# Second attention divided behind its value products, and the first mixer's sigmoids read from the banks

## The chip, the core and the metric

The program runs on one core of a Trainium2 chip. The metric is the device time of one execution in microseconds (us), lower is better. A core has a matrix engine (TensorE, PE in the profile, with its weight loads as PEld), three engines for elementwise work (VectorE or DVE, ScalarE or ACT, GpSimd or POOL), and a queue that issues the transfers (SyncE or SP). The matrix engine writes into eight banks of 128 x 512 f32. Each engine works through its own instructions in order and meets the others only at semaphores.

## What is computed

Two transformer blocks run one after the other on 512 tokens of width 1024. The first has a gated FFN, a token mixer (four recurrent heads, `_hgrn2`, beside a spatial gating), a cross attention over 256 memory tokens, and a second FFN. The second block has a mixer of self attention and pooling, and an FFN. Two pieces are touched.

The gates of the first mixer, in the reference:

```
log_f = jnp.log(lb + (1.0 - lb) * jax.nn.sigmoid(fz))
k = (1.0 - lb) * jax.nn.sigmoid(-fz)
b = jnp.cumsum(lfc, axis=2)            # within chunks
```

The self attention of the second block, 8 query heads of 64 over 2 key and value heads:

```
s = jnp.einsum('bqkgd,bskd->bkgqs', qblk, k).astype(jnp.float32) * scale
p = jax.nn.softmax(s, axis=-1)
return jnp.einsum('bkgqs,bskd->bqkgd', p.astype(v.dtype), v)
```

## The kernel before

**Linear layers.** Each weight is used as a high part (`whi`, cast by ScalarE, L394) and a low part (`wlo`, a subtraction by VectorE or GpSimd, L399; `lo_owner` at L359 says by which). A block is 128 output columns: eight products with the high part and the high activation (L434), eight with the low activation (L435), and eight with the low part of the weight (L438). Blocks run through banks 0 to 3. Each block has a place in one list (`blocks`), and the casts and splits run three blocks ahead (`AHEAD`).

**First mixer.** Its input layer (`in`, 24 blocks) begins with the four forget projections FZ0 to FZ3, which are multiplied in halves together with the layer norm in front. `plan` (L660) lists for each block which small steps follow it; each engine has a function `mixer` with its own part of each step. For a head: VectorE copies the bank to `mk` (L1787). ScalarE takes two sigmoids of it, L1059 into `cum` and L1060 into `mk`. VectorE makes forget gate and key (L1694 to L1696). ScalarE takes the logarithm (L1065, after `use_logs`, L1001, which loads another table). VectorE scans (L1700). GpSimd makes the arguments of the decays (L1298, L1299) and ScalarE their exponential (L1069). VectorE scales query and key by them (L1665 into `qt`, L1667 into `kt`), and the matrix engine multiplies these (L2206), for 7 levels and the diagonal. The first two such products stand behind block 5 (IV0) in the matrix engine's order, the next two behind block 6, and so on.

VectorE's order at the start, before: copies of blocks 0 to 2, between them the low parts of blocks 4 and 5; the gates of head 0 ahead of the copy of block 3; then the gates of heads 1, 2 and 3, the scan of head 0, the copy of block 4 (Q0), and the first scaling. GpSimd splits block 6 at its step 3 and block 7 at its step 4, behind the arguments of levels 0 and 1.

**Second attention.** Before its loop the layer `in2` (10 blocks) makes keys, queries, values and the pooled input; the scores of head 0 stand behind block 8. In turn h of the loop the matrix engine does: scores of tiles 0 and 1 of head h+1 (L2369, L2370); transposes of columns 0 and 1 of head h's probabilities (`self_turn`, L2418); scores 2; value products 0 and 1 of head h-1 (`self_attend`, L2430); scores 3; transposes 2 and 3; value products 2 and 3. In turns 2 to 5 the product of one pooling group follows (L2453). VectorE takes each tile's maximum (L1903), ScalarE the exponential with the row's sum (L1177), and VectorE inverts the sum (L1911) and multiplies the probabilities by it in place (L1912). Only then are they transposed (wait on `s_pn`). VectorE copies one transposed column out of the bank (L1964), ScalarE three (L1211). The value product of a head fills 64 of a bank's 128 partitions, so two heads share a bank; after the second of them ScalarE writes the high part `ahi` (L1217) and VectorE the low part `alo` (L1969), both from the bank. `out2` takes these tiles in the order `OUT2_TILES`. GpSimd pools (L1348 to L1352) during the first turns.

Of the kernel before, what the change touches and what calls it, by code (L numbers as in the profile page):

```python
# [92 lines left out]
def build(nc, A, out):  # L93
    ctx = ExitStack()
    with ctx:
# [116 lines left out]
        sv = take("sv", [P, TT, P])  # L212
# [6 lines left out]
        po = rope  # L219
        take = region(0)  # L220
# [352 lines left out]
        s_sig = sem("gates_sigmoid")  # L573
# [54 lines left out]
        s_ah = sem("attended_hi")  # L628

# [31 lines left out]
        for h in range(HG):  # L661
            plan[1 + h] += [("forget", h)]
        plan[4] += [("logs", 0)]
# [81 lines left out]
        OUT2_TILES = [0, 7, 1, 6, 5, 2, 4, 3]  # L745
# [101 lines left out]
        def _(act):  # L847
# [208 lines left out]
            def mixer(kind, n):  # L1056
                if kind == "forget":
                    wait_in(act, FZ0 + n)
                    link(act.activation(cum[:, n, :], mk[:, n, :], ACT.Sigmoid))  # L1059
                    act.activation(mk[:, n, :], mk[:, n, :], ACT.Sigmoid, scale=-1.0).then_inc(s_sig, 1)  # L1060
                elif kind == "logs":
                    use_logs()
                    for h in range(HG):
                        act.wait_ge(s_fg, h + 1)
                        act.activation(cum[:, h, :], cum[:, h, :], ACT.Ln).then_inc(s_lf, 1)  # L1065
# [103 lines left out]
            def self_exp(h, t):  # L1169
# [7 lines left out]
                act.activation(ps[:, h % 2, t, :], score_bank(n)[:, :], ACT.Exp, bias=small[:, c:c + 1],  # L1177
                               accum_out=small[:, S_SM + n % 8:S_SM + n % 8 + 1]).then_inc(s_pe, 1)
# [33 lines left out]

            def attended_hi(h):

                if h % 2:
                    act.wait_ge(s_pv, 2 * XH + h + 1)
                    act.copy(ahi[:, h // 2, :], bank[6 + (h // 2) % 2][:, :]).then_inc(s_ah, 1)  # L1217

            for h in range(QH):
                if h >= 2:  # L1220
                    attended_hi(h - 2)
                self_exp(h + 1, 0)
                self_exp(h + 1, 1)
                if 0 <= h - POOL_AT - 1 < 4:
# [3 lines left out]
                take_transposed(h, 1)  # L1228
                self_exp(h + 1, 2)
                self_exp(h + 1, 3)  # L1230
                take_transposed(h, 2)
                take_transposed(h, 3)
# [125 lines left out]
        def _(dve):  # L1358
# [330 lines left out]
            def mixer(kind, n):  # L1689
                if kind == "forget":  # L1690

                    lb, oml = small[:, S_LB + n:S_LB + n + 1], small[:, S_OML + n:S_OML + n + 1]
                    dve.wait_ge(s_sig, n + 1)
# [76 lines left out]
            GATES = {3: (("forget", 0),), 4: (("forget", 1), ("forget", 2), ("forget", 3), ("scan", 0))}  # L1770
# [5 lines left out]
            for n, tasks in enumerate(plan):  # L1776
                for task in GATES.get(n, ()):
                    mixer(*task)
                for task in tasks:
                    if task[0] not in ("forget", "logs"):  # L1780
# [5 lines left out]
                wait_block(dve, phases["in"], n)  # L1786
                dve.tensor_copy(IN_DST[n], bank_of(phases["in"], n)[:, :]).then_inc(bank_free, 1)  # L1787
# [117 lines left out]
            def self_normalise(h, t):  # L1905
                n = TT * h + t
                c = n % 8
                if h >= QH:
                    return
                dve.wait_ge(s_pe, TT * XH + n + 1)  # L1910
                link(dve.reciprocal(small[:, S_RI + c:S_RI + c + 1], small[:, S_SM + c:S_SM + c + 1]))  # L1911
                dve.tensor_scalar(ps[:, h % 2, t, :], ps[:, h % 2, t, :], small[:, S_RI + c:S_RI + c + 1], None, ALU.mult).then_inc(s_pn, 1)  # L1912

            def prepare(kind, j):
                if kind == "softmax":
                    for t in range(TT):
                        self_max(0, t)
                        if t:
# [556 lines left out]
```

## Time and profile before

| | |
|---|---|
| median of three runs | 1740.86 us (1740.73 to 1741.76) |
| the profiled execution | 1740.76 us, of which its span is 1738.9 us |
| busy in the span | PE 1701.5 us (98%), DVE 681.1 (39%), ACT 589.5 (34%), POOL 710.9 (41%) |
| mean granted clock of the matrix engine | 0.996 |
| longest waits of the matrix engine for another engine | 4.1 us in the first mixer, 3.4 us in the second attention |

The busy share of a matrix engine's row counts matmuls at a lower clock as busy, too. In a timeline, rows of one line that follow each other are merged (x8), the time behind them runs to the end of the last, and matmuls overlap: the start of the next row tells how long the engine was taken. Square brackets give the idle time before a row and what ended it.

### The profile page before, as it was taken

The page shows a single profiled execution, that of the slowest core. Times are in us where ns is not written, and L with a number is a line of the kernel's source. Part 1 is how long each engine was busy: PE and PEld are TensorE (multiplying, and loading weights), DVE is VectorE, ACT ScalarE, POOL GpSimd, SP SyncE. Part 2 cuts the span into 40 slices and gives each one's busy share as a digit, 9 for nine tenths or more (in the row PEclk, how much of TensorE's full clock was granted, in tenths as well). Part 3 has the DMA queues.
Part 4 walks back from the last instruction along what each step waited for, and adds up shares of the span by engine and source line. Part 5 has one row for each costly group of instructions (what it writes and reads, how often), then busy time and mean ns, then how long its engine had stood idle before and what let it go on. Part 6 is the DMA issues. An engine that isn't in the chain of part 4 may idle for free.

```text
span 1738.9 us, 21093 instructions
## 1 busy us (share of the span) xinstructions
PE 1701.5 (98%) x8525; PEld 1417.6 (82%) x8525; DVE 681.1 (39%) x1122; ACT 589.5 (34%) x890; POOL 710.9 (41%) x386
## 2 busy tenths in 40 slices
PE   7999999998999999999999999999899999999998
PEld 6888888897888789879888888898657988888886
DVE  3111211268776776356211121266884522112122
ACT  4222222256444554236222222246453422222210
POOL 3443444445554343114453444433331454444442
PEclk9999999999999999999999999999999999999999
DMA  6333243333222345212433233342111333323322
GB/s 189 97 97 97 79 116 97 97 110 85 61 61 61 97 125 142 73 49 71 112 97 97 82 112 97 86 128 61 37 37 49 85 98 97 97 82 112 97 85 73
DMA packets 302826, 157.66 MB, mean 91 GB/s; under 512 B 5145, under 2 KB 301194, under 8 KB 302730
## 3 DMA queue, kind: packets, MB, share of 16 engines
q1 hardware_dynamic: 302730, 156.32, 31.6%
q8 instruction: 68, 1.11, 0.3%
q14 instruction: 28, 0.23, 0.1%
HBM read 154.20 MB, written 2.10 MB: 90 GB/s over the span
## 4 chain that ended last, share of the span: by engine, by line
PE 66%; DVE 4%; ACT 3%; issue 2%; POOL 0%; DVEq 0%; ACTq 0%; POOLq 0%
PE bank L434 16%; PE bank L435 16%; PE bank L438 15%; PE bank L2430 1%; PE bank L2054 1%; PE bank L2051 1%; PE bank L2050 1%; PE bank L481 1%; PE bank L482 1%; PE bank L486 1%; PE bank L2206 1%; PE bank L467 1%; PE bank L461 1%; PE bank L462 1%; PE bank L2311 1%
## 5 line engine op out<-in xcount | busy, mean ns | idle before, releaser
L399 POOL TENSOR_TENSOR wlo<-wraw,whi 128x1024 fp32r<-128x1024 f32 (+1 forms) x256 | 608.6, 2390 | 909.9 <-ACT whi L394 909.9
L434 PE MATMUL bank<-ahi,whi 128*128 128x512 f32 x1312 | 516.0, 393 | 0.0
L435 PE MATMUL bank<-alo,whi 128*128 128x512 f32 x1312 | 511.7, 390 | 0.0
L394 ACT CAST whi<-wraw 128x1024 fp32r<-128x1024 f32 (+1 forms) x286 | 285.9, 1025 | 255.4 <-PE bank L438 169.4
L438 PE MATMUL bank<-ahi,wlo 128*128 128x512 f32 x1312 | 324.0, 389 | 0.0
L434 PEld LDWEIGHTS bank<-ahi,whi 128*128 128x128 f32 x1312 | 247.2, 188 | 52.1 <-issue 1.2
L435 PEld LDWEIGHTS bank<-alo,whi 128*128 128x128 f32 x1312 | 247.0, 188 | 52.0 <-issue 1.2
L438 PEld LDWEIGHTS bank<-ahi,wlo 128*128 128x128 f32 x1312 | 246.3, 188 | 51.1
L1377 DVE SCALAR_TENSOR_TENSOR hval<-gate,bank 128x512 f32<-128x512 f32 x66 | 45.4, 688 | 557.2 <-PE bank L438 543.2
L859 ACT ACTIVATE gate<-bank 128x512 f32<-128x512 f32 x66 | 39.6, 600 | 514.9 <-PE bank L438 506.1
L1386 DVE SCALAR_TENSOR_TENSOR res<-res,bank 128x512 f32<-128x512 f32 x80 | 54.1, 686 | 261.7 <-PE bank L438 181.7
L434 PE MATMUL bank<-hid,whi 128*128 128x512 f32 x332 | 130.5, 393 | 0.0
L435 PE MATMUL bank<-hid,whi 128*128 128x512 f32 x332 | 129.9, 391 | 0.0
L438 PE MATMUL bank<-hid,wlo 128*128 128x512 f32 x332 | 83.4, 391 | 0.0
L438 PEld LDWEIGHTS bank<-hid,wlo 128*128 128x128 f32 x332 | 62.3, 188 | 13.7
L434 PEld LDWEIGHTS bank<-hid,whi 128*128 128x128 f32 x332 | 62.4, 188 | 13.4
L435 PEld LDWEIGHTS bank<-hid,whi 128*128 128x128 f32 x332 | 62.4, 188 | 13.4
L1368 DVE TENSOR_TENSOR hid<-hval,hid 128x512 fp32r<-128x512 f32 x66 | 67.2, 1019 | 2.3
L876 ACT ACTIVATE gate<-res 128x256 f32<-128x256 f32 (+1 forms) x48 | 23.4, 488 | 120.5 <-DVE res L1386 66.7
L2050 PE MATMUL bank<-ahi,whi 128*128 128x256 f32 x256 | 63.3, 285 | 0.0
L2051 PE MATMUL bank<-alo,whi 128*128 128x256 f32 x256 | 62.8, 283 | 0.0
L481 PE MATMUL bank<-hid,whi 128*128 128x512 f32 x132 | 52.0, 394 | 0.0
(304 smaller groups left out, 2241.7 us busy)
## 6 DMA issues: line engine op xcount, KB each, us to landing
wraw<-in_ffn_w_gate SPq DMA_DIRECT2D x44, 512.0 KB, 3.8
wraw<-in_ffn_w_up SPq DMA_DIRECT2D x44, 512.0 KB, 3.8
wraw<-in_w_in SPq DMA_DIRECT2D x34, 512.0 KB, 3.9
wraw<-in_ffn_w_down SPq DMA_DIRECT2D x32, 512.0 KB, 4.0
wraw<-in_w_gate SPq DMA_DIRECT2D x22, 512.0 KB, 3.8
wraw<-in_w_up SPq DMA_DIRECT2D x22, 512.0 KB, 3.8
wraw<-in_w_out SPq DMA_DIRECT2D x16, 512.0 KB, 4.4
wraw<-in_w_down SPq DMA_DIRECT2D x16, 512.0 KB, 4.0
```

Source lines behind the costliest of these rows:

```text
L394: eng.copy(whi[:, b % 4, 0:n], wraw[:, b % RAW, 0:n]).then_inc(hi_ready, 1)
L399: eng.tensor_tensor(wlo[:, b % RAW, 0:n], wraw[:, b % RAW, 0:n], whi[:, b % 4, 0:n], ALU.subtract).then_inc(LO[b][0], 1)
L434: eng.matmul(o, w, xhi[:, k, :], start=(k == 0), stop=False)
L435: eng.matmul(o, w, xlo[:, k, :], start=False, stop=False)
L438: mm = eng.matmul(o, wlo[:, b % RAW, k * P:(k + 1) * P], xhi[:, k, :], start=False, stop=(k == ph.K - 1))
L481: eng.matmul(o, whi[:, b % 4, k * P:(k + 1) * P], hhi[:, k, :], start=(k == 0), stop=False)
L859: act.activation(gate[:, tile % 2, :], bank_of(ph, j)[:, :], ACT.Silu).then_inc(gate_done, 1)
L1368: dve.tensor_tensor(hlo[:, at, :], hval[:, tile % 2, :], hhi[:, at, :], ALU.subtract).then_inc(hidden_ready, 1)
L1377: dve.scalar_tensor_tensor(out=hval[:, tile % 2, :], in0=gate[:, tile % 2, :], scalar=scale, in1=bank_of(ph, j)[:, :], op0=ALU.mult, op1=A ...
L1386: dve.scalar_tensor_tensor(out=res[:, j, :], in0=res[:, j, :], scalar=scale, in1=bank_of(ph, j)[:, :], op0=ALU.mult, op1=ALU.add).then_inc ...
L2050: pe.matmul(o, w, xhi[:, k, at], start=(k == 0), stop=False)
L2051: pe.matmul(o, w, xlo[:, k, at], start=False, stop=False)
```

## The change

Second attention: the probabilities are transposed as they come out of the exponential, with no row sum and no division. The values are laid out in five slots of 64 columns per tile, `sv`: ones, values of group 0, ones, values of group 1, ones. A value product takes two neighbouring slots as its stationary operand, 128 columns rather than 64, and leaves the 64 sums beside the 64 attended rows, on the other half of the partitions (`rows_of`). Each head has a bank of its own (6 or 7 in turn). ScalarE inverts the sums as exp(-ln), in two instructions on 64 x 512 (`invert_sums`), VectorE multiplies (`divide`) into `ao`, and the high and low parts are made from `ao`. The tile of pooling is handled later in a turn on both engines, and `OUT2_TILES` follows the new order. First mixer: ScalarE reads the sigmoids of the four forget blocks from the banks and frees them; VectorE's four copies are gone. The logarithms of heads 0 to 2 come behind the gates of head 3, that of head 3 one step later, and VectorE scans head 0 ahead of the gates of head 3. ScalarE casts blocks 6 and 7 behind the sigmoids rather than ahead of them, and the low part of block 6 goes from GpSimd to VectorE.

```diff
-        sv = take("sv", [P, TT, P])
+        sv = take("sv", [P, TT, 5, HD])
-            return DVE if b == 1 or b - phases["in"].base in (4, 5) or (b % 2 and blocks[b][0].name in DVE_SPLITS) else POOL
+            return DVE if b == 1 or b - phases["in"].base in (4, 5, 6) or (b % 2 and blocks[b][0].name in DVE_SPLITS) else POOL
-        for h in range(HG):
-            plan[1 + h] += [("forget", h)]
-        plan[4] += [("logs", 0)]
+        plan[1] += [("forget", 0)]
+        plan[2] += [("forget", 1)]
+        plan[3] += [("forget", 2)]
+        plan[4] += [("forget", 3), ("log", 0), ("log", 1), ("log", 2)]
+        plan[5] += [("log", 3)]
-        OUT2_TILES = [0, 7, 1, 6, 5, 2, 4, 3]
+        OUT2_TILES = [0, 7, 6, 1, 5, 4, 2, 3]
...
                 if kind == "forget":
-                    wait_in(act, FZ0 + n)
-                    link(act.activation(cum[:, n, :], mk[:, n, :], ACT.Sigmoid))
-                    act.activation(mk[:, n, :], mk[:, n, :], ACT.Sigmoid, scale=-1.0).then_inc(s_sig, 1)
+                    at = bank_of(phases["in"], n)[:, :]
+                    wait_block(act, phases["in"], n)
+                    act.activation(cum[:, n, :], at, ACT.Sigmoid)
+                    act.activation(mk[:, n, :], at, ACT.Sigmoid, scale=-1.0).then_inc(bank_free, 1)
...
-                if 1 <= n <= 4:
+                if 1 <= n <= 2:
                     hi_stream(phases["in"], n)
                 for task in tasks:
                     mixer(*task)
-                if n > 4:
+                if n > 2:
                     hi_stream(phases["in"], n)
...
+            def invert_sums(h):
+
+                own, other = rows_of(h)
+                act.wait_ge(s_pv, 2 * XH + h + 1)
+                if h >= 2:
+                    act.wait_ge(s_pn, TT * XH + h - 1)
+                link(act.activation(rinv[other, h % 2, :], bank[6 + h % 2][other, :], ACT.Ln))
+                act.activation(rinv[own, h % 2, :], rinv[other, h % 2, :], ACT.Exp, scale=-1.0).then_inc(s_si, 1)
...
             for h in range(QH):
                 if h >= 2:
-                    attended_hi(h - 2)
+                    invert_sums(h - 2)
                 self_exp(h + 1, 0)
                 self_exp(h + 1, 1)
+                take_transposed(h, 1)
+                self_exp(h + 1, 2)
+                self_exp(h + 1, 3)
+                if h >= 2:
+                    attended_hi(h - 2)
+                take_transposed(h, 2)
+                take_transposed(h, 3)
...
+            invert_sums(QH - 2)
+            invert_sums(QH - 1)
             attended_hi(QH - 1)
...
-            GATES = {3: (("forget", 0),), 4: (("forget", 1), ("forget", 2), ("forget", 3), ("scan", 0))}
+            GATES = {2: (("forget", 0),), 3: (("forget", 1),), 4: (("forget", 2), ("scan", 0), ("forget", 3))}
...
-                wait_block(dve, phases["in"], n)
-                dve.tensor_copy(IN_DST[n], bank_of(phases["in"], n)[:, :]).then_inc(bank_free, 1)
+                if n >= 4:
+                    wait_block(dve, phases["in"], n)
+                    dve.tensor_copy(IN_DST[n], bank_of(phases["in"], n)[:, :]).then_inc(bank_free, 1)
...
                 if j == 6:
+                    link(dve.memset(sv[:, :, 0:5:2, :], 1.0))
...
+            def divide(h):
+                own, other = rows_of(h)
+                dve.wait_ge(s_si, h + 1)
+                dve.tensor_tensor(ao[own, (h // 2) % 2, :], bank[6 + h % 2][own, :], rinv[own, h % 2, :], ALU.mult).then_inc(s_pn, 1)
...
             for h in range(QH):
-                self_normalise(h, TT - 1)
                 self_max(h + 1, 0)
                 self_max(h + 1, 1)
+                take_transposed(h, 0)
                 if h >= 2:
-                    attended_lo(h - 2)
+                    divide(h - 2)
+                self_max(h + 1, 2)
+                self_max(h + 1, 3)
...
-                    pe.wait_ge(s_pn, TT * XH + TT * (h + 1))
+                    pe.wait_ge(s_pe, TT * XH + TT * (h + 1))
...
-                    if h >= 4 and h % 2 == 0:
-                        pe.wait_ge(*operand("out2", OUT2_TILES.index(h // 2 - 2)))
-                i = pe.matmul(bank[6 + (h // 2) % 2][p0:p0 + HD, :], sv[:, st, HD * (h // 4):HD * (h // 4) + HD],
-                              psT[:, h % 2, st, :], start=(st == 0), stop=(st == TT - 1))
+                    if h >= 2:
+                        pe.wait_ge(s_pn, TT * XH + h - 1)
+                n = 2 * (h // 4) + (h + 1) % 2
+                i = pe.matmul(bank[6 + h % 2][:, :], sv[:, st, n:n + 2, :], psT[:, h % 2, st, :], start=(st == 0), stop=(st == TT - 1))
```

## Rows read from the trace of the kernel before

**Rows 1.** The page, part 1: busy us, share of the span, instructions.
```profile
PE 1701.5 (98%) x8525; PEld 1417.6 (82%) x8525; DVE 681.1 (39%) x1122; ACT 589.5 (34%) x890; POOL 710.9 (41%) x386
```
**Rows 2.** Waits of the matrix engine: line, awaited, us in total, times, longest.
```profile
PE bank L2206 <- DVE kt L1667: 5.4, 3, 4.1
...
PE bank L2418 <- DVE ps L1912: 4.7, 3, 3.4
```
**Rows 3.** Timeline, PE, first mixer: start us, us, engine, line, operation [idle before].
```profile
414.18 1.98 PE L438 MATMUL bank<-ahi,wlo 128*128 128x512 f32 x8
420.27 3.68 PE L2206 MATMUL bank<-qt,kt 128*128 128x64 f32 x16 [4.12 <-DVE kt L1667]
...
430.87 1.89 PE L2206 MATMUL bank<-qt,kt 128*128 128x64 f32 x16
```
**Rows 4.** Windows: stretch, length, busy us and instructions by engine, clock, DMA.
```profile
488.20:491.60 3.40, 2.08 (x17) 1.88 (x17) 3.33 (x10) 0.00 (x0) 0.00 (x0) 1.00 0.54 154
491.60:495.00 3.40, 3.38 (x18) 3.40 (x19) 1.95 (x4) 0.00 (x0) 0.00 (x0) 0.55 0.02 5
...
1276.20:1284.80 8.60, 8.60 (x36) 4.45 (x35) 7.01 (x16) 5.85 (x15) 0.00 (x0) 1.00 0.00 1
```
**Rows 5.** Timeline, ACT, first mixer.
```profile
401.82 0.63 ACT L1059 ACTIVATE cum<-mk 128x512 f32<-128x512 f32 x1
...
403.02 1.03 ACT L394 CAST whi<-wraw 128x1024 fp32r<-128x1024 f32 x1
...
410.91 1.28 ACT L1001 ACT_TABLE_LOAD   x1
412.21 2.34 ACT L1065 ACTIVATE cum<-cum 128x512 f32<-128x512 f32 x4
```
**Rows 6.** Timeline, DVE, first mixer.
```profile
404.08 1.22 DVE L399 TENSOR_TENSOR wlo<-wraw,whi 128x1024 fp32r<-128x1024 f32 x1 [0.98 <-ACT whi L394]
...
406.26 2.70 DVE L1696 TENSOR_SCALAR mk<-mk,small 128x512 f32<-128x512 f32 x1
...
412.35 0.54 DVE L1694 TENSOR_SCALAR cum<-cum,small 128x512 f32<-128x512 f32 x1
...
413.80 1.22 DVE L1700 TENSOR_TENSOR_SCAN cum<-restart,cum 128x512 f32<-128x512 f32 x1
...
417.65 2.57 DVE L1667 TENSOR_TENSOR kt<-mk,dec 128x256 f32<-128x256 f32 x1
```
**Rows 7.** Timeline, POOL, first mixer.
```profile
415.09 0.62 POOL L1298 TENSOR_TENSOR dec<-cum 128x256 f32<-128x256 f32 x1 [6.42 <-DVE cum L1700]
...
417.40 2.53 POOL L399 TENSOR_TENSOR wlo<-wraw,whi 128x1024 fp32r<-128x1024 f32 x1
```
**Rows 8.** Timeline, PE, second attention.
```profile
1250.63 0.47 PE L2369 MATMUL bank<-khi,sst 128*128 128x512 f32 x1 [0.88 <-DVE su L1956]
...
1252.87 1.77 PE L2418 MATMUL bank<-mats,ps 128*128 128x128 f32 x8 [1.09 <-DVE ps L1912]
...
1261.73 1.09 PE L2418 MATMUL bank<-mats,ps 128*128 128x128 f32 x8 [3.42 <-DVE ps L1912]
...
1268.47 0.50 PE L2369 MATMUL bank<-khi,sst 128*128 128x512 f32 x1
...
1269.52 1.03 PE L2418 MATMUL bank<-mats,ps 128*128 128x128 f32 x8
...
1270.95 1.93 PE L2430 MATMUL bank<-psT,sv 128*64 128x512 f32 x4
```
**Rows 9.** Timeline, DVE, second attention.
```profile
1250.59 2.23 DVE L1912 TENSOR_SCALAR ps<-ps,small 128x512 f32<-128x512 f32 x1
...
1277.83 1.29 DVE L1903 TENSOR_REDUCE small<-bank 128x1 f32<-128x512 f32 x2 [1.19 <-PE bank L2370]
```
**Rows 10.** Timeline, ACT, second attention.
```profile
1278.56 0.69 ACT L1177 ACTIVATE ps<-bank,small 128x512 f32<-128x512 f32 x1 [1.18 <-DVE small L1903]
```
**Rows 11.** Groups by form, PE, 700 to 760 us: the cross attention's value products.
```profile
L2336 PE MATMUL bank<-pxT,vx 128*128 128x512 f32 x32 | 14.2, 592 | 0.0
```

More of the change, by code:

```diff
@@ L219, in build @@
         po = rope
+        take = region(WORK + 84 * KB)
+        rinv = take("rinv", [P, 2, T])
+        ao = take("ao", [P, 2, T])
         take = region(0)
@@ L628, in build @@
         s_ah = sem("attended_hi")
+        s_si = sem("sums_inverted")
         s_rope = sem("rope_loaded")
@@ L744, in build, with rows_of @@
         LN2_AT = {3: 0, 5: 1, 7: 2, 9: 3, 11: 4, 12: 5, 13: 6, 15: 7}
-        OUT2_TILES = [0, 7, 1, 6, 5, 2, 4, 3]
+        def rows_of(h):
+            return slice(HD * (h % 2), HD * (h % 2) + HD), slice(HD * (1 - h % 2), HD * (1 - h % 2) + HD)
+        OUT2_TILES = [0, 7, 6, 1, 5, 4, 2, 3]
         def last_block_in(ph, b):
@@ L1057, in mixer @@
                 if kind == "forget":
-                    wait_in(act, FZ0 + n)
-                    link(act.activation(cum[:, n, :], mk[:, n, :], ACT.Sigmoid))
-                    act.activation(mk[:, n, :], mk[:, n, :], ACT.Sigmoid, scale=-1.0).then_inc(s_sig, 1)
[L1061 to L1065, printed above, removed]
+                    at = bank_of(phases["in"], n)[:, :]
+                    wait_block(act, phases["in"], n)
+                    act.activation(cum[:, n, :], at, ACT.Sigmoid)
+                    act.activation(mk[:, n, :], at, ACT.Sigmoid, scale=-1.0).then_inc(bank_free, 1)
+                elif kind == "log":
+                    if n == 0:
+                        use_logs()
+                    act.wait_ge(s_fg, n + 1)
+                    act.activation(cum[:, n, :], cum[:, n, :], ACT.Ln).then_inc(s_lf, 1)
                 elif kind == "level" and n in NTH:
@@ L1176, in self_exp @@
                 c = S_NM + n % 8
[L1177 to L1178 removed]
+                act.activation(ps[:, h % 2, t, :], score_bank(n)[:, :], ACT.Exp, bias=small[:, c:c + 1]).then_inc(s_pe, 1)
             def prepare(kind, j):
@@ L1211, in take_transposed @@
                 act.copy(psT[:, h % 2, st, :], bank[3 + st % 2][:, :]).then_inc(s_pca, 1)
+            def invert_sums(h):
[5 more added lines that the diff above has]
+                act.activation(rinv[own, h % 2, :], rinv[other, h % 2, :], ACT.Exp, scale=-1.0).then_inc(s_si, 1)
             def attended_hi(h):
                 if h % 2:
-                    act.wait_ge(s_pv, 2 * XH + h + 1)
-                    act.copy(ahi[:, h // 2, :], bank[6 + (h // 2) % 2][:, :]).then_inc(s_ah, 1)
+                    act.wait_ge(s_pn, TT * XH + h + 1)
+                    act.copy(ahi[:, h // 2, :], ao[:, (h // 2) % 2, :]).then_inc(s_ah, 1)
             for h in range(QH):
                 if h >= 2:
-                    attended_hi(h - 2)
+                    invert_sums(h - 2)
                 self_exp(h + 1, 0)
                 self_exp(h + 1, 1)
+                take_transposed(h, 1)
[5 more added lines that the diff above has]
+                take_transposed(h, 3)
                 if 0 <= h - POOL_AT - 1 < 4:
@@ L1779, in _ @@
                 for task in tasks:
-                    if task[0] not in ("forget", "logs"):
+                    if task[0] not in ("forget", "log"):
                         mixer(*task)
@@ L1935, in prepare @@
                     dve.wait_ge(s_svT, 1)
-                    dve.tensor_copy(sv[:, :, :], bank[7][:, :].rearrange("p (n f) -> p n f", f=P)).then_inc(s_dupc, 1)
+                    dve.tensor_copy(sv[:, :, 1:5:2, :], bank[7][:, :].rearrange("p (n g f) -> p n g f", g=2, f=HD)).then_inc(s_dupc, 1)
                 elif kind == "take_k":
@@ L1990, in _ @@
                                       ALU.add, ALU.mult).then_inc(s_py, 1)
-                take_transposed(h, 0)
-                self_max(h + 1, 2)
-                self_normalise(h + 1, 0)
-                self_normalise(h + 1, 1)
-                self_max(h + 1, 3)
-                self_normalise(h + 1, 2)
+                if 0 <= h - POOL_AT - 2 < 4:
+                    n = h - POOL_AT - 2
+                    dve.wait_ge(s_pyh, n + 1)
+                    g = POOL_ORDER[n]
+                    dve.tensor_tensor(alo[:, 4 + g, :], po[:, n % 2, :], ahi[:, 4 + g, :], ALU.subtract).then_inc(act_dve, 1)
+                if h >= 2:
+                    attended_lo(h - 2)
+            divide(QH - 2)
+            divide(QH - 1)
             attended_lo(QH - 1)
```

27 lines of the change are left out of this document (3 added, 24 removed).

## The prediction, made before the changed kernel was run

> **What bounds the kernel now.** I read the page's first part: the matrix engine is busy for 98% of the span [rows 1], so only its gaps, its slow stretches and its instruction count matter. Its own waits come next [rows 2]: two of the longest stand where the diff works, for `kt` (L1667) in the first mixer and for the divided probabilities (L1912) in the second attention. The timeline of the engine then places them [rows 3, 8]; the timelines of the other three tell what ended last [rows 5 to 7, 9, 10]; the windows give the clock [rows 4].
>
> **Second attention, what goes.** After the last input block the engine waits 0.88 us for a bank, does two score tiles, and stands 1.09 us until VectorE has divided the last tile of head 0. That division took 2.23 us, beside GpSimd's pooling. In turn 1 it waits 3.42 us for the same thing, and a third such wait is what is left of the 4.7 us: 0.2 [rows 2, 8, 9]. After the second gap eight transposes took 1.77 us, against 1.03 later [rows 8]: a fall to the lower of the two levels, 1.2 GHz, as in the window at a clock of 0.55 [rows 4].
>
> Now the transposes wait for the exponentials alone, and those of head 0 are over long before. With lengths from the later rows: a pair of score tiles 1.05 from its start to the transposes (1268.47 to 1269.52), a pair of transposes 1.0 [rows 8]. Turn 0 starts at 1250.63 as before, and the transposes at 1251.7. Next come score 2 (0.5), score 3 (0.5; its bank needs the exponential of tile (1,0), below), transposes 2 and 3 (1.0), and scores 0 and 1 of turn 1 (0.9), so that the transposes of head 1 are reached at 1255.5. What they wait for goes through the other engines: score (1,0) is there at 1251.4; the maximum takes 0.6 and starts the exponential 0.73 after its own start (1277.83 to 1278.56) [rows 9, 10], at 1252.1. ScalarE then has exponentials (1,0) and (1,1), a column copy, (1,2) and (1,3), the last at 1254.7 to 1255.3 since its score ends at 1253.8 and its maximum at 1254.5, and two more column copies of 0.5 each, the first of which frees the bank at 1255.8. So the transposes start at 1255.9 where they started at 1261.73. From there to turn 2 the engine has 6.7 us of work without a gap (1261.73 to 1268.47 [rows 8]), and it has the same. **Gain 5.8 us, and 0.2 for the third wait: 6.0.** The 0.88 us stays: nothing in the diff moves that bank's copy.
>
> **What comes.** (a) Stationary operands of 128 columns instead of 64: the cross attention's products are such, 592 ns each and 14.2 us for 32, 0.44 apiece [rows 11]; the value products here are four in 1.93, of which the last runs on [rows 8], 0.43 to 0.46. Cost nothing; bounds -1 and +1 us over 64. (b) Per head two ScalarE instructions of about 0.6 (a logarithm is 0.585 in a row of four [rows 5]), with the wait between them 1.3 us, and one VectorE multiply of 0.7. They stand at the head of a turn, behind the last value product. The exponentials queued behind them could start only after a pooling product (0.9), a score tile (0.5) and a maximum, some 2.2 us later, or 1.4 without a pooling product: covered. ScalarE is busy for 5.85 of a turn of 8.6 us, VectorE for 7.0 [rows 4]; ScalarE comes to about 6.8, and VectorE falls, since four divisions and reciprocals go for one multiply. (c) The value products of head h now wait for the division of head h-2. That is made in turn h and asked for in turn h+1: cover of most of a turn. (d) At the end, logarithm, exponential, multiply, cast and subtraction take 3.3 us after the last product, where `out2` takes the last tile eighth of eight; seven tiles of six matmuls at 0.23 are 9.5 us. Covered. ScalarE's next weight cast comes 1.5 us later and is wanted after 9.5 us, too. (e) Moving the pooled tile: on VectorE it passes one copy and two maxima, on ScalarE three copies; the order of `OUT2_TILES` follows and no tile before the last is made in the last microseconds. Nothing. (f) The memset of ones (768 elements a partition) has no row: it lies between nothing and the 1.22 of a 512 element scan [rows 6]. It counts only where the matrix engine waits for VectorE behind it, and its one gap up to the loop, 0.88, follows a copy that came two blocks later [rows 8]. I take nothing, and 0.4 us as its bound on the path.
>
> **First mixer, what goes.** The chain into the 4.12 us gap: VectorE makes the four gates, 1.45 us each (412.35 to 413.80), scans at 413.80, GpSimd starts the arguments at 415.09, the exponential follows, and VectorE's `kt` at 417.65 takes 2.57 us since GpSimd has begun the split of block 7 at 417.40, 2.53 us long; `kt` ends with it. The products start at 420.27, at half speed: 3.68 us for what takes 1.89 one step later [rows 3, 5 to 7]. The block before ended at 416.0 (eight matmuls from 414.18, 0.23 apart).
>
> The new chain, step by step. ScalarE starts the sigmoids at 401.82 as now, since its table load and the cast ahead of it stay. Four pairs at 1.15 (1.2 apart from 401.82 to 403.02, less the wait between the two, which goes) and two casts at 0.95 (1.03, overlapping) end at 408.3, the table of logarithms at 409.6, the first logarithm at 410.2. VectorE meanwhile has, from 403.0 on, three gates (4.35) and the splits of blocks 5 and 6 (2.4, at 1.22 each [rows 6]): 409.8. It no longer loses the 2.2 us of the `mk` product that took 2.70 [rows 6] beside GpSimd's split of block 6: that split is VectorE's own now, and costs 1.2. So the scan starts at 410.3, **3.5 us earlier**. Arguments of level 0 start at 411.6. Here is the new queue: ScalarE has the logarithm of head 3 ahead of the first exponential, and it waits for the gates of head 3, which VectorE makes behind the scan (411.4 to 412.9, or to 413.6 if GpSimd's arguments hold them up). The first exponential ends at 414.1 to 414.8. By then GpSimd is through with two levels (2.3 to 3.0 us from 411.6) and has begun the split of block 7, so the first scaling is again held until that ends, at 416.3 to 417.1, and `kt` needs 0.8 more. Products from 417.3 to 418.0; I take 417.7. Level 0 takes 0.9, level 1 waits 0.7 for its operands (1.5 us behind level 0's) and takes 0.9. Block 6 runs from 420.2 for 5.5 (24 matmuls, of which eight take 1.8) and level 2 starts at 425.7, where it started at 430.87. Gain 5.2. Two steps later VectorE, which gained some 0.8 less than the matrix engine, has a slack of about 0.6; I take off 0.2. **Gain 5.0 us** at the full clock, of which 2.6 is idle time and the rest clock.
>
> The Trainium skill (ScalarE: Activation LUTs, What ACT_TABLE_LOAD costs) puts a switch of table at 2.66 us with its drain. Here the load is 1.28 and the logarithm starts 0.02 after it [rows 5]; by the page's figure the scan would start 1.4 us later and the mixer's gain would be some 3.6.
>
> **The sum.** 1740.76 (span 1738.9 and 1.9 around it) less 6.0 and 5.0 is 1729.8. The median of the runs shown is 0.1 above the profiled run: 1729.9.
>
> **Rivals.** *A: the clock falls anyway.* The mixer keeps about 2.4 us of gaps between short products. A stretch like that, 2.08 busy of 3.40 us and mostly such products, was followed by one at a clock of 0.55; the transposes behind the gap of 3.42, at 1.09 for eight, ran at the higher level [rows 8]. A fall costs half of 3.4 us, 1.7; in the attention's first turns, with 0.88 idle and short transposes, another 1.7 could go. One fall gives 1731.6, both 1733.3. Chance of one or both 0.33. The Trainium skill (TensorE: Matmul & The Clock Gate, Part 1) has the monitor run free of the program, so that one kernel can meet a fall in one run and none in another.
>
> *B: the mixer gives its gain back.* VectorE and GpSimd collide through the next steps, as `kt` does now, and the products of levels 2 to 6 wait for what the first two no longer wait for. For it: VectorE is at work without much pause there, and its chain gains 2.6 to 3.5, not 5. Against: the matrix engine has no gap there now. Only the 2.6 stay: 1732.3. Chance 0.15.
>
> *C: ScalarE becomes the bound of a turn; the other side.* Place: the head of each turn, between logarithm and exponential. If each of the two, and the rows' exponentials behind them, had to load its own table, an inversion would be 1.3 + 3 x 1.28 = 5.1 us, ScalarE's turn 6.8 + 3.8 = 10.6 and seven turns 2.0 longer each, 14, with some falls of the clock (1.7 each, two): 1747. It decides from 3.1 us per inversion on (8.6 - 6.8 + 1.3), and makes the kernel slower than before from 4.7 on (11 us over 7 turns). Against: the four logarithms and the exponentials after them show one load [rows 5]. Chance 0.03. The Trainium skill (ScalarE: Activation LUTs, Table sets: the hidden batching unit) has ln and exp in one set, which by its rule excludes C.
>
> *D: nothing much.* The engine is held in turn 1 and in the mixer by something hidden behind the division and behind `kt`: the columns' copies, or the values' layout. Some 3 of the 11 us are gained: 1738. Chance 0.05.
>
> **Chances and range.** Forecast 0.44, A 0.33, B 0.15, D 0.05, C 0.03. The forecast's own range, from the bounds of (a), (f) and the two ends of the mixer's start, is 1728.2 to 1731.5. For 8 in 10 I reach over A and B and leave out C and D: 1727.5 to 1734.5. A measurement of this kernel can tell 0.2%, 3.5 us, from no change; faster is 0.92 (forecast, A and B), the same 0.05 (D), slower 0.03.
>
> **What would show it.** Right: the wait for L1912 is gone, the one transposition wait left is a few tenths for L1211, in turn 1; turn 2 starts some 5.8 us sooner after the last input block; later turns last 8.6 us as before; the `kt` gap is 1.3 to 2.1 us, with a second of 0.7 behind it, and the split of block 7 still overlaps `kt`; the scan starts 3.5 us earlier. Wrong: a gap at the head of later turns (C), a granted clock of 0.5 in 416 to 424 or 1250 to 1257 (A), new waits for L1665 or L1667 at levels 2 to 6 (B), a wait for `psT` or `sv` (D).

## The result, and the profile after

| | before | after |
|---|---|---|
| median of six runs, us | 1740.80 (1740.36 to 1741.76) | 1726.38 (1725.29 to 1726.71) |
| the profiled execution, us | 1740.76 | 1725.29, of which its span is 1723.5 |
| ratio of the times, 95% interval | | 0.9915, 0.9905 to 0.9925 |

The kernel is faster by 14.4 us, 0.8%, where 10.9 us were forecast. 1726.38 lies 1.1 us below the low end of the range, 1727.5. The profiled execution is the fastest of the six, 1.1 below their median, so what is read from it below adds up to 15.4 us of span.

The page of the changed kernel, part 1:

```profile
PE 1693.5 (98%) x8525; PEld 1420.4 (82%) x8525; DVE 659.2 (38%) x1064; ACT 594.7 (35%) x874; POOL 708.0 (41%) x385
```

Beside [rows 1] the matrix engine's busy time falls by 8.0 us with the same 8525 instructions. Removed waits alone cannot do that: either the clock was higher for longer, or instructions have become cheaper.

Waits of the matrix engine, changed kernel: line, awaited, us in total, times, longest.

```profile
PE bank L2223 <- DVE kt L1688: 3.0, 4, 1.3
...
PE bank L2386 <- DVE su L1968: 0.9, 1, 0.9
...
PE bank L2435 <- ACT psT L1220: 0.3, 1, 0.3
```

Against [rows 2] the waits of 4.7 us for divided probabilities are gone. What is left of them is 0.3 for a column's copy, as the prediction said. For `kt` 3.0 are left of 5.4.

**The second attention.** Timeline, PE, changed kernel, the first score behind the last input block, the transposes of head 1, and two pooling products:

```profile
1245.14 0.47 PE L2386 MATMUL bank<-khi,sst 128*128 128x512 f32 x1 [0.88 <-DVE su L1968]
...
1250.30 1.07 PE L2435 MATMUL bank<-mats,ps 128*128 128x128 f32 x8 [0.30 <-ACT psT L1220]
...
1263.49 1.02 PE L2469 MATMUL bank<-su,poolw 128*128 128x512 f32 x2
...
1271.38 1.02 PE L2469 MATMUL bank<-su,poolw 128*128 128x512 f32 x2
```

The transposes of head 1 come 5.16 us after the first score (1245.14 to 1250.30), where 11.10 passed before (1250.63 to 1261.73 [rows 8]): 5.9 gained for a forecast of 5.8. But a turn, measured from pooling product to pooling product, lasts 7.89 us (1263.49 to 1271.38). Before it lasted 8.6, and the prediction left it there.

**The first mixer.** Timeline, PE, changed kernel, and the window behind it (stretch, length, busy us and instructions of PE, PEld, DVE, ACT and POOL, granted clock, DMA share, GB/s):

```profile
417.37 1.10 PE L2223 MATMUL bank<-qt,kt 128*128 128x64 f32 x8 [1.30 <-DVE kt L1688]
418.91 1.10 PE L2223 MATMUL bank<-qt,kt 128*128 128x64 f32 x8 [0.44 <-DVE kt L1688]
...
422.15 0.63 PE L437 MATMUL bank<-ahi,whi 128*128 128x512 f32 x1
...
426.98 1.89 PE L2223 MATMUL bank<-qt,kt 128*128 128x64 f32 x16
```
```profile
420.20:423.60 3.40, 3.40 (x10) 2.63 (x9) 3.27 (x7) 0.77 (x1) 3.40 (x3) 0.51 0.00 0
```

The gap of 4.12 [rows 3] has become one of 1.30 and one of 0.44. Level 2 starts at 426.98 where it started at 430.87: 3.9 us earlier, for a forecast of 5.2. Behind the two gaps the clock fell to its lower level, 1.2 GHz (0.51 in the window; products of 0.63 rather than 0.39).

**Where the 15.4 us of span went.** From the first score behind the last input block to the second product of `out2`, the attention takes 58.8 us (1245.14 to 1303.91), where it took 68.8 (1250.63 to 1319.40): 10.0. Up to that first score 5.5 are gained (1250.63 to 1245.14). Behind the attention nothing changed: 419.5 us before, 419.6 after. The stage of the attention repeats well from trace to trace (58.8 us in the changed kernel and in the four below that also have two runs of 128 columns in a turn and no division), so it prices an edit there better than the medians do.

### The profile page after: what moved, and what is told of

It reads as the page before. It is cut to its first block, busy times and chain, and to the rows that moved or that the text cites. A ratio compares the mean times of both kernels' runs of the same rounds, so it can differ in the third digit from the quotient of the medians.

```text
span 1723.5 us, 21024 instructions
## 1 busy us (share of the span) xinstructions
PE 1693.5 (98%) x8525; PEld 1420.4 (82%) x8525; DVE 659.2 (38%) x1064; ACT 594.7 (35%) x874; POOL 708.0 (41%) x385
## 4 chain that ended last, share of the span: by engine, by line
PE 88%; DVE 4%; ACT 4%; issue 2%; DMA 0%; POOL 0%; SPq 0%; DVEq 0%; ACTq 0%; POOLq 0%
PE bank L438 21%; PE bank L437 21%; PE bank L441 21%; PE bank L484 2%; PE bank L485 2%; PE bank L489 2%; PE bank L2068 2%; PE bank L2071 2%; PE bank L2067 2%; PE bank L2447 2%; PE bank L470 1%; PE bank L464 1%; PE bank L465 1%; PE bank L2223 1%; ACT res L908 1%
## 5 line engine op out<-in xcount | busy, mean ns | idle before, releaser
L438 PEld LDWEIGHTS bank<-hid,whi 128*128 128x128 f32 x332 | 62.5, 188 | 13.3
```

Of the source, the lines that this page charges most:

```text
L438: eng.matmul(o, w, xlo[:, k, :], start=False, stop=False)
```

## Experiments

The question was, above all, where the surplus of some 4 us in the attention comes from. Two theories: **width** (a value product with 128 stationary columns is cheaper where it stands than one with 64), and **order** (the new sequence of the turn does it, through waits that overlap differently).

### Width alone, in the kernel before

```diff
-                i = pe.matmul(bank[6 + (h // 2) % 2][p0:p0 + HD, :], sv[:, st, HD * (h // 4):HD * (h // 4) + HD],
+                i = pe.matmul(bank[6 + (h // 2) % 2][:, :], sv[:, st, :],
```

The second head of a pair overwrites the first, so the result is wrong; everything else is done as before.

> The kernel before with one edit: the value products of the second attention take all 128 value columns as their stationary operand instead of the 64 of their group, and fill the whole bank. The second head of each pair so overwrites the first, and the attended rows are wrong; nothing is left out in time. Width theory (the 64-column operand costs at the change from and to 128-column ones, about 0.33 us a pair of products, two pairs a turn): turns 2 to 5 last 7.9 us instead of 8.6, the three waits for the division stay, and the time is some 5 us lower, 1735.8. Order theory (turns got shorter in the changed kernel because the waits on the division and the shared bank are gone, not by width): turns of 8.6 us, 1740.8.

Measured: 1738.20 beside 1740.91, ratio 0.9982 (0.9973 to 0.9992). Faster, by 2.7 us. Of its turns 3 to 5, from one pooling product to the next, two last 7.9 us and one 8.1, against 8.6 before. So the width acts alone, with all waits of the old order in place, and the theory of order, which expects turns of 8.6 here, falls. Timeline, PE, this kernel, turn 1:

```profile
1259.84 1.09 PE L2418 MATMUL bank<-mats,ps 128*128 128x128 f32 x8 [3.53 <-DVE ps L1912]
...
1261.39 3.41 PE L2430 MATMUL bank<-psT,sv 128*128 128x512 f32 x4
```

Four rows, which are two products, took 3.41 us for 1.88 in the changed kernel: behind the gap of 3.53 the clock fell, which it had not done in the trace of before. From these transposes to the second score product of turn 2 it took 8.1 us, for 6.4 in the changed kernel: 1.7 us which this trace loses and that of before does not. The third wait for a division grew, too, from 0.16 to 0.64. The whole stage lasts 67.7 us, 1.1 less than the 68.8 before: the 3.8 that the width is worth (worked out below) less 1.7, 0.5 and some 0.3 in two longer turns is 1.3. The other 1.9 of the 3.0 between the two profiled executions lie ahead of the stage, where the programs are alike. So the length of the turns shows the effect of the width; that the medians differ by 2.7 prices nothing.

### Width alone taken back, in the kernel after

```diff
-                link(act.activation(rinv[other, h % 2, :], bank[6 + h % 2][other, :], ACT.Ln))
+                link(act.activation(rinv[other, h % 2, :], bank[6 + h % 2][own, :], ACT.Square))
...
-                n = 2 * (h // 4) + (h + 1) % 2
-                i = pe.matmul(bank[6 + h % 2][:, :], sv[:, st, n:n + 2, :], psT[:, h % 2, st, :], start=(st == 0), stop=(st == TT - 1))
+                own = rows_of(h)[0]
+                i = pe.matmul(bank[6 + h % 2][own, :], sv[:, st, 2 * (h // 4) + 1, :], psT[:, h % 2, st, :], start=(st == 0), stop=(st == TT - 1))
```

The row sums are left out, so the result is wrong; ScalarE and VectorE do as many instructions as before on other values.

> The changed kernel with 64-column value products again, each head into its own half of its own bank. The sums are left out: the first ScalarE instruction squares the attended rows instead of taking the logarithm of the sums, so count and sizes of the instructions stay and only the result is wrong. Width theory: turns of 8.6 us again, some 5 us over the changed kernel, 1731.4. Order theory: turns of 7.9 us stay, 1726.4.

Measured: 1730.40 beside 1740.91, ratio 0.9938 (0.9921 to 0.9954). It is 4.0 us slower than the changed kernel, which is the size of the surplus. The stage lasts 62.5 us here for 58.8 in the changed kernel, 3.8 more. Timeline, PE, this kernel, one run of value products between two scores:

```profile
1268.69 0.39 PE L2387 MATMUL bank<-klo,sst 128*128 128x512 f32 x1
1269.01 1.93 PE L2447 MATMUL bank<-psT,sv 128*64 128x512 f32 x4
1270.87 0.50 PE L2386 MATMUL bank<-khi,sst 128*128 128x512 f32 x1
1271.21 0.39 PE L2387 MATMUL bank<-klo,sst 128*128 128x512 f32 x1
```

The same place in the changed kernel:

```profile
1274.27 0.40 PE L2387 MATMUL bank<-klo,sst 128*128 128x512 f32 x1
1274.50 1.88 PE L2447 MATMUL bank<-psT,sv 128*128 128x512 f32 x4
1275.82 0.80 PE L2386 MATMUL bank<-khi,sst 128*128 128x512 f32 x1
1276.45 0.39 PE L2387 MATMUL bank<-klo,sst 128*128 128x512 f32 x1
```

From the score ahead of the run to the second score behind it: 2.52 us (1268.69 to 1271.21) against 2.18 (1274.27 to 1276.45), 0.34 more for 64 columns. The rows of the products themselves read 1.93 and 1.88. The difference sits at the borders: the first 64-column product starts 0.32 behind the score rather than 0.23, and the score behind the run starts only near the run's end (1.86 after its start), where with 128 columns it starts after 1.32 and most of it lies beside the last product. A turn has two runs, and twice 0.34 is, to rounding, the 0.67 by which its turns are longer (8.57 for 7.90).

### Each half of the change alone

The mixer's edits alone in the kernel before:

```diff
-        for h in range(HG):
-            plan[1 + h] += [("forget", h)]
...
+        plan[4] += [("forget", 3), ("log", 0), ("log", 1), ("log", 2)]
```

> The mixer's part of the change alone. My account of the two traces: the products of levels 0 and 1 start 2.9 us earlier and level 2 some 3.8 us earlier; the lower clock two steps later (1.7 us in the trace of before) comes or stays away by chance. So 1735.4 to 1737.0. As predicted before the result: 5.0 us, 1735.8. Rival B of the prediction (gain given back by later waits): 1738.2.

Measured: 1735.98 beside 1740.91, ratio 0.9970 (0.9957 to 0.9983): 4.9 us. The gaps are 1.31 and 0.43, and the clock falls behind them, as in the whole. In its trace, too, the fall at 491.60 to 495.00 [rows 4] is absent, of which more below, so that not all of the 4.9 is the mixer's own.

The attention's edits alone:

```diff
-                    pe.wait_ge(s_pn, TT * XH + TT * (h + 1))
+                    pe.wait_ge(s_pe, TT * XH + TT * (h + 1))
```

> The attention's part of the change alone. Width theory: 6 us from the division's waits, as predicted, and some 4 to 5 from the width of the value products: 1730.5. If the surplus over the prediction is the mixer's: 1734.8 (6.0 us alone).

Measured: 1729.63 beside 1740.91, ratio 0.9933 (0.9918 to 0.9947): 11.3 us, where 6.0 were predicted for this half. Its stage lasts 58.8 us, as in the changed kernel, 10.0 less than before. Here the gap in the mixer is 4.12 as in [rows 3]. The two halves add up to 16.2 for 14.4 in the whole; with intervals of some 2.5 us to either side of each that is no disagreement, nor a proof that they are independent.

### Is it each product, or the change of width?

If every 64-column product were dearer, putting a turn's value products (four, each of two rows in the trace, so x8) into one run would not help. If the cost is one for each run, it halves. The same edit, in the narrow kernel above and in the changed one:

```diff
                 self_scores(h + 1, 2)
-                self_attend(h - 1, 0)
-                self_attend(h - 1, 1)
                 self_scores(h + 1, 3)
...
                 self_turn(h, 3)
+                self_attend(h - 1, 0)
+                self_attend(h - 1, 1)
                 self_attend(h - 1, 2)
```

Narrow, in one run:

> The 64-column value products of e2_narrow (sums left out, so a wrong result), with all four of a turn in a row behind the last transposes instead of two and two. Switch theory (a fixed cost where the stationary operand changes between 64 and 128 columns, none inside a run of equal ones): one entry and one exit a turn instead of two, turns of 8.24 us instead of 8.57. Per product theory (each 64-column product is slower in itself): 8.57 stays.

Measured: one execution, 1727.91. Timeline, PE, a run, the pooling products around a turn, and the last run of the stage:

```profile
1264.85 1.13 PE L2469 MATMUL bank<-su,poolw 128*128 128x512 f32 x2
...
1269.59 3.65 PE L2447 MATMUL bank<-psT,sv 128*64 128x512 f32 x8
1273.17 1.13 PE L2469 MATMUL bank<-su,poolw 128*128 128x512 f32 x2
...
1300.79 5.42 PE L2447 MATMUL bank<-psT,sv 128*64 128x512 f32 x16
```

Wide, in one run:

> The changed kernel (128-column value products, all of its work) with the four value products of a turn in a row behind the last transposes, as e6_narrow_together had them with 64 columns (turns of 8.33 us there against 8.57). Switch theory (the 0.24 saved there is one entry into and one exit from 64 columns less): here nothing changes width, turns stay at 7.9 us and the time at 1726.4. Rival (joining any two runs of value products saves it, whatever their width): turns of 7.65 us, some 1.7 us less, 1724.7.

Measured: 1727.51 beside 1740.51, ratio 0.9926 (0.9911 to 0.9941), 1.1 above the changed kernel. Timeline, PE:

```profile
1264.40 1.02 PE L2469 MATMUL bank<-su,poolw 128*128 128x512 f32 x2
...
1268.95 3.60 PE L2447 MATMUL bank<-psT,sv 128*128 128x512 f32 x8
1272.39 1.02 PE L2469 MATMUL bank<-su,poolw 128*128 128x512 f32 x2
...
1297.74 1.39 PE L2435 MATMUL bank<-mats,ps 128*128 128x128 f32 x8 [0.35 <-DVE psT L1976]
1298.96 7.03 PE L2447 MATMUL bank<-psT,sv 128*128 128x512 f32 x16
```

The four turns side by side, in us:

| | two runs in a turn | one run in a turn |
|---|---|---|
| 64 columns | 8.57 | 8.33 |
| 128 columns | 7.90 | 7.99 |
| difference | 0.67 | 0.34 |

The difference follows the number of runs and not the number of products, which is the same in all four. So it is a price for going from 128-column operands to 64 and back: some 0.33 us for each run. The order alone costs 0.09 at 128 columns; 0.33 saved less 0.09 is the 0.24 by which the narrow turn became shorter. Both kernels with one run also have a new gap of 0.35 in turn 7. The wide one's stage lasts 60.2 us instead of 58.8, so for the changed kernel it is no gain.

### What holds the mixer's gap

Theory: `qt` and `kt` wait for GpSimd's split of block 7. Rival: the arguments and exponentials themselves are late. The first try gives the split to VectorE:

```diff
-            return DVE if b == 1 or b - phases["in"].base in (4, 5, 6) or (b % 2 and blocks[b][0].name in DVE_SPLITS) else POOL
+            return DVE if b == 1 or b - phases["in"].base in (4, 5, 6, 7) or (b % 2 and blocks[b][0].name in DVE_SPLITS) else POOL
```

> The changed kernel with one more weight split (block 7 of the first mixer's input) moved from GpSimd to VectorE, where it takes 1.2 us ahead of the first scaling. Collision theory (the first scaling is held until GpSimd's 2.4 us split ends, and the lower clock behind it comes from the two gaps): scaling done by 415.9, gaps of 1.3 and 0.4 us gone, and with them the fall of the clock, 1.7: 1723.0. If the fall comes without the gaps: 1724.7. Chain theory (the gap is the length of the chain gates, scan, arguments, exponential, and would be there without the split): kt no earlier, 1726.4 or up to 1 us more.

Measured: 1723.89 beside 1740.98, ratio 0.9905 (0.9888 to 0.9921), 2.5 below the changed kernel. Timelines of DVE and PE, this kernel:

```profile
412.95 1.62 DVE L402 TENSOR_TENSOR wlo<-wraw,whi 128x1024 fp32r<-128x1024 f32 x1
414.49 0.83 DVE L1686 TENSOR_TENSOR qt<-mq,dec 128x256 f32<-128x256 f32 x1
415.25 0.86 DVE L1688 TENSOR_TENSOR kt<-mk,dec 128x256 f32<-128x256 f32 x1
```
```profile
416.17 2.19 PE L2223 MATMUL bank<-qt,kt 128*128 128x64 f32 x16 [0.54 <-DVE kt L1688]
...
423.75 1.89 PE L2223 MATMUL bank<-qt,kt 128*128 128x64 f32 x16
...
440.07 1.10 PE L2223 MATMUL bank<-qt,kt 128*128 128x64 f32 x8 [0.98 <-DVE kt L1688]
```

VectorE does the split in 1.62 and is still earlier with `kt`. One gap of 0.54 is left, where the theory expected none; the clock did not fall, and level 2 starts 3.2 us earlier than in the changed kernel. A new gap of 0.98 gives 1.1 of that back, and the time lies 0.9 above the 1723.0 expected.

The second try leaves the split on GpSimd and lets the first exponential pass the logarithm of head 3:

```diff
-        plan[5] += [("log", 3)]
...
                 plan[g0 + 2] += [("take_values", h)]
+        plan[5] += [("log", 3)]
```

> The changed kernel with the logarithm of head 3 behind the first two exponentials on ScalarE instead of ahead of them. Queue theory of the prediction (the first exponential waits for that logarithm and through it for the gates of head 3): the exponential starts at 412.7 instead of 413.4, the first scaling at 413.5, before GpSimd's split of block 7 starts at 413.9. If VectorE then keeps its turn for both products, kt ends by 414.4 and the time is as with the split moved away, 1723.0 to 1724.7. If GpSimd gets in between the two, kt still ends with its split at 416.3 and the time is 1725.5 to 1726.4.

Measured: 1725.67 beside 1740.98, ratio 0.9913 (0.9898 to 0.9928), 0.7 below the changed kernel, which such runs do not tell from nothing. Timelines of DVE, POOL and PE, this kernel:

```profile
413.52 0.71 DVE L1686 TENSOR_TENSOR qt<-mq,dec 128x256 f32<-128x256 f32 x1
414.15 2.62 DVE L1688 TENSOR_TENSOR kt<-mk,dec 128x256 f32<-128x256 f32 x1
```
```profile
413.91 2.58 POOL L402 TENSOR_TENSOR wlo<-wraw,whi 128x1024 fp32r<-128x1024 f32 x1
```
```profile
416.83 1.10 PE L2223 MATMUL bank<-qt,kt 128*128 128x64 f32 x8 [0.76 <-DVE kt L1688]
...
441.73 1.10 PE L2223 MATMUL bank<-qt,kt 128*128 128x64 f32 x8 [1.54 <-DVE kt L1688]
```

`qt` now starts 0.6 us earlier, ahead of the split, but GpSimd began the split at 413.91, while `qt` ran and before `kt` started. `kt` then took 2.62, to the end of the split. The exponential was a part of the lateness, the split is what decides. Behind gaps of 0.76 and 0.43 the clock did not fall in this trace, and level 2 starts 2.1 us earlier than in the changed kernel; the new gap of 1.54 gives most of that back.

### The two findings in one kernel

The split of block 7 on VectorE as above, and the scores of the attention's turns begin in bank 2 rather than in bank 1, which holds the last input block; that is aimed at the wait of 0.88:

```diff
-            return bank[(5, 4, 6, 7)[n] if n < TT else n % 3]
+            return bank[(5, 4, 6, 7)[n] if n < TT else (n + 1) % 3]
```

> The split of block 7 on VectorE as in e5_split7, and the scores of heads 1 to 7 go through banks 2, 0, 1 instead of 1, 2, 0, so that the first score behind the last input block does not wait for that block's bank. Theory: the 0.88 us wait goes and everything behind it starts 0.9 us earlier: 0.9 us under e5_split7, 1722.1. Rival: the wait moves to the third score, or to the transposes of turn 0, and nothing is gained: as e5_split7.

Measured: 1722.82 beside 1740.98, ratio 0.9897 (0.9882 to 0.9912). This is the lowest median of the study, 3.6 us below the changed kernel. The 1.1 by which it lies below the kernel with the split alone is less than such runs tell apart; between the two traces the matrix engine gains 0.9 at the first score and keeps it to the end of the stage. Timeline, PE, the same place as `1245.14` above:

```profile
1241.04 1.98 PE L441 MATMUL bank<-ahi,wlo 128*128 128x512 f32 x8
1242.85 0.39 PE L2386 MATMUL bank<-khi,sst 128*128 128x512 f32 x1
```

The first score follows the last block without a gap. The wait of 0.88 has no successor of its size: only the 0.30 for a column's copy is left in the stage.

The same with a turn's value products in one run:

> e9_best with the four value products together. Switch theory: as e9_best, 1722.8. Rival: 1.7 us less, 1721.1.

Measured: 1724.09 beside 1740.51, ratio 0.9905 (0.9888 to 0.9921), 1.3 above the kernel without it, and its stage lasts 60.2 us for 58.8. As in the wide kernel above, there is no change of width left to save.

## Why the prediction was wrong where it was

**The step that failed: (a), the width of the stationary operands.** I took nothing for it, with bounds of one us either way. It is worth 3.8: from the transposes of head 1 to the second product of `out2`, the narrow kernel takes 57.4 us and the changed one 53.6. Turns 1 to 5 give 0.68 each, 3.4 in all; turns 6 and 7, where scores and with them borders are missing, 1.0; and 0.65 are lost at the end. There the kernel before has a run across two heads (12 rows, PE, kernel before):

```profile
1314.63 4.51 PE L2430 MATMUL bank<-psT,sv 128*64 128x512 f32 x12
...
1319.40 0.40 PE L462 MATMUL bank<-ahi,wlo 128*128 128x512 f32 x1
```

and the changed kernel:

```profile
1298.53 5.32 PE L2447 MATMUL bank<-psT,sv 128*128 128x512 f32 x12
...
1303.91 0.40 PE L465 MATMUL bank<-ahi,wlo 128*128 128x512 f32 x1
```

4.77 against 5.38 us to the second product of the layer: here the narrow ones are the faster, and the narrow kernel has the same, 4.73. Taken one by one, the rows of the narrow run start 0.4 to 0.5 apart, as everywhere, except at the border between the heads, where two pairs start together (1315.52 and 1315.54, then 1315.97 twice). Products of two heads go to different halves of the partitions. The narrow kernel with one run in a turn has eight rows of each head in its last run: four pairs start together there, and 16 rows take 5.42 us, against 7.03 for wide ones. Runs of one head, narrow or wide, have no such pair, nor have wide ones across a head. So narrow products of different halves do run side by side; why only these rows pair up is open.

The surplus of the attention is then accounted for: 10.0 is 5.9 for the first two turns (5.8 predicted), 3.8 for the width and 0.3 for the rest, of which the third wait is 0.16 (0.2 predicted). The mistake was in the reading. I compared the length of the rows (592 ns each [rows 11], 1.93 for four [rows 8]), and the price lies between the rows. Starts had to be compared, from the instruction ahead of a run to the second one behind it. What [rows 8] show is not enough: they give 1.93 for the run, but no start of what follows. In the trace of before the score behind that run starts 1.86 after it (1270.95 to 1272.81), where four rows 0.43 apart, as the wide ones are, would be 1.72. Nor could [rows 11] bound the term: they show 128-column products among their like, with no change of width at all.

The Trainium skill (TensorEngine Tiling (Array Packing), Key Properties) states that changing the tiling mode drains the matrix engine, and that different tiles can work in parallel; by its section When to Use Tiling, an operand of up to 64 columns is one that column tiling is for. The trace agrees with both, with 0.33 us a run for the first and the pairs at the border of two heads for the second; that a 64-column operand sets another mode is my reading, as no row names a mode. The page gives no price, and I had not weighed it.

**The waits of the attention: right.** The first two turns gained 5.9 for 5.8, and with 0.3 of the rest the term of 6.0 came out at 6.2. The remaining wait is 0.30 for L1220, in turn 1, as said. The 0.88 stayed.

**The covers of (b) to (f): right.** The inversion in turn 2 of the changed kernel, ACT:

```profile
1256.65 0.59 ACT L1228 ACTIVATE rinv<-bank 64x512 f32<-64x512 f32 x1 [0.22 <-PE bank L2447]
1257.27 0.63 ACT L1229 ACTIVATE rinv<-rinv 64x512 f32<-64x512 f32 x1
1257.93 1.26 ACT L1187 ACTIVATE ps<-bank,small 128x512 f32<-128x512 f32 x2
```

1.25 us for the two, the exponentials right behind them and no load of a table between: rival C did not happen. In a turn (1271.38 to 1279.27) ScalarE was busy for 6.3 us, where I had 6.8, and VectorE for 5.3. The memset took 0.70, at 1223.2, far ahead of the loop. No wait of the matrix engine names the inversion, the division, `ao` or the memset.

**The mixer: the chain right, the clock wrong.** This is the second step that failed, and 1.6 us in size. Timelines of DVE, ACT and POOL, changed kernel:

```profile
409.68 1.23 DVE L1721 TENSOR_TENSOR_SCAN cum<-restart,cum 128x512 f32<-128x512 f32 x1
...
414.13 2.42 DVE L1686 TENSOR_TENSOR qt<-mq,dec 128x256 f32<-128x256 f32 x1 [0.68 <-DVE mq L1809]
416.48 0.83 DVE L1688 TENSOR_TENSOR kt<-mk,dec 128x256 f32<-128x256 f32 x1
```
```profile
408.94 1.68 ACT L1075 ACTIVATE cum<-cum 128x512 f32<-128x512 f32 x3
...
413.43 1.16 ACT L1079 ACTIVATE dec<-dec 128x512 f32<-128x512 f32 x2
```
```profile
413.88 2.39 POOL L402 TENSOR_TENSOR wlo<-wraw,whi 128x1024 fp32r<-128x1024 f32 x1
```

The scan started at 409.68 (forecast 410.3), the scaling was held by the split until 416.5, and the products started at 417.37 (forecast 417.7). My gain of 5.0 was also labelled wrongly: 2.6 was how much earlier the products would start, while by the gaps that I forecast (1.3 to 2.1, and 0.7) only 1.3 to 2.1 of it was idle time; 2.4 were measured (4.12 less 1.74). The forecast's likeliest case kept the clock; rival A, at 0.33, had it fall, and it fell. Nine products from 420.13 took 3.65 where nine take 2.06 at 0.23 apiece: 1.6 us, priced at 1.7. Without that, level 2 would stand at 425.4, for 425.7 forecast.

It was made good elsewhere. The fall at 491.60 to 495.00 [rows 4] is absent in the changed kernel's trace (window, changed kernel):

```profile
491.60:495.00 3.40, 3.40 (x16) 2.81 (x15) 2.62 (x2) 2.71 (x4) 3.40 (x4) 1.00 0.00 0
```

That is 1.6 more. Against it stands a fall which the changed kernel's trace has and that of before has not (window, changed kernel):

```profile
1171.20:1174.60 3.40, 3.40 (x18) 3.40 (x17) 2.81 (x8) 2.83 (x7) 1.77 (x3) 0.50 0.01 2
```

It cost 1.4, and 1.3 of that came back 9 us later, where the matrix engine before had waited for ScalarE's `squares` and now had not. So 3.9 and 1.6 are the 5.5 that reach the attention, within 0.1.

Neither fall can be claimed for the change. The one near 490 stands in all three traces with the old mixer (before, width alone, attention alone) and in two of the nine with the new one; one of these is the narrow kernel's, whose program is the changed kernel's up to there, with a clock of 0.67 at 488.20 to 491.60. That leans to the change, but each kernel has one trace. So the medians' 4.9 for the mixer's half, for a forecast of 5.0, is in part luck: up to level 2 the change gained 3.9, and the fall that stayed away filled the rest. Rival B, the gain given back at later levels, did not decide, but it is real: when the first gap shrank further, gaps of 0.98 and 1.54 came up at 440 to 442.

**The sum.** 1729.9 less 3.8 for the width is 1726.1, and what is left to the median of 1726.38, 0.3, is less than the spread of the runs. In the profiled execution the 1.6 near 490 more than make up for the mixer's 3.9 where 5.0 were forecast, which is luck and not foresight.

## What to carry to other kernels

Between matmuls, compare starts, not lengths: from the instruction ahead of a group to the second one behind it, in the same kernel. A stationary operand of 64 columns among ones of 128 cost a third of a us for each group here (moving operands of 512 columns, f32), so put such products together, or fill the other 64 columns with something useful, as the sums are here. Narrow products for the two halves of the partitions, one behind the other, ran in part side by side; a kernel built on that was not tried. Before a VectorE product with two operands in SBUF, look at what GpSimd starts at that moment, not only at what the product waits for.

## What was new of the hardware

- Going from 128-column stationary operands to 64 and back cost 0.34 us for each run of f32 products of 512 columns (turns of 8.57 and 7.90 with two runs, 8.33 and 7.99 with one).
- At the border between two heads, whose narrow products go to different halves of the partitions, rows started in pairs: 12 rows in 4.51 us against 5.32 for wide ones (two pairs), 16 rows in 5.42 against 7.03 (four pairs).
- VectorE can lose its turn between two of its own instructions. `qt` took 0.71 from 413.52, GpSimd's split began at 413.91, and `kt` behind it took 2.62 instead of 0.8. The Trainium skill (SBUF — State Buffer, Who interferes with whom) has VectorE with two SBUF inputs and a GpSimd instruction that reads SBUF exclude each other for a whole instruction. The traces agree in the main: each time the product ended within 0.3 us of the split, though the rows of the split and of the `qt` ahead of it overlap by 0.3.
